# GpSimd waits for VectorE's candidate sums between two of its trees, and three columns of the up-projection move from the end of the selection into the gate table's stage

## The reference: what is computed

```python
def peer_ffn(xn, w_query, sub_keys, expert_u, expert_v):    # for each block of 128 tokens, xb
    q = (xb @ w_query).reshape(c, 8, 2, 128)                 # 8 heads, 2 halves
    s = einsum('chpd,pkd->chpk', q, sub_keys)                # 128 scores per head and half
    s_top, i_top = top_k(s, 16)
    cand = s_top[:, :, 0, :, None] + s_top[:, :, 1, None, :] # sums of pairs
    best, pos = top_k(cand, 16)                              # 16 experts per head
    idx = (i_top half 0 * 128 + i_top half 1) at pos
    g = softmax(best)
    act = gelu(einsum('chkd,cd->chk', expert_u[idx], xb))
    return einsum('chk,chkd->cd', g * act, expert_v[idx])
```

## Time and profile before

| | |
|---|---|
| median of three runs | 3433.51 us |
| the profiled execution: span | 3434.3 us |
| PE busy | 3377.4 us, 98% |
| DVE busy | 2636.7 us, 77% |
| ACT busy | 1240.8 us, 36% |
| POOL busy | 809.2 us, 24% |
| chain that ended last | PE 81%, DVE 14%, DMA 2% |

### The profile page before, as it was taken

How to read it: one execution, slowest core, us unless ns; L and a number is a source line. 1 busy time by engine, 2 the same in 40 slices (tenths; PEclk the granted TensorE clock), 3 DMA queues, 4 the chain that set the end, 5 groups by cost and what they waited for, 6 DMA issues and landing times.

```text
span 3434.3 us, 47304 instructions
## 1 busy us (share of the span) xinstructions
PE 3377.4 (98%) x16086; PEld 2755.3 (80%) x16086; DVE 2636.7 (77%) x5503; ACT 1240.8 (36%) x1980; POOL 809.2 (24%) x661
## 2 busy tenths in 40 slices
PE   7999999999999999999999999999999999999998
PEld 4458855898889988888855688559988888898887
DVE  3574389997888888888736734999978888888888
ACT  2333223794223233333214322339833333222332
POOL 0000026002333333333300000440033333333332
PEclk9999999999999999999999999999999999999999
DMA  4313313468888888888741132144698888888885
GB/s 122 104 37 92 119 37 123 161 254 315 319 304 303 305 304 306 306 308 307 259 159 37 37 103 101 44 140 181 246 354 308 309 308 304 302 306 306 304 305 202
DMA packets 270646, 750.58 MB, mean 219 GB/s; under 512 B 19741, under 2 KB 139293, under 8 KB 243904
## 3 DMA queue, kind: packets, MB, share of 16 engines
q1 hardware_dynamic: 196768, 480.57, 39.7%
q0 software_dynamic: 73760, 268.47, 22.7%
HBM read 681.86 MB, written 67.11 MB: 218 GB/s over the span
## 4 chain that ended last, share of the span: by engine, by line
PE 81%; DVE 14%; DMA 2%; POOL 1%; ACT 1%; issue 1%; SPq 0%; DVEq 0%; POOLq 0%; ACTq 0%
PE ps L1239 29%; PE ps L1225 22%; PE ps L1029 7%; PE ps L898 4%; PE ps L1122 4%; DVE OHS L2143 3%; PE ps L1087 3%; PE ps L876 2%; DVE OHS L2139 2%; PE ps L1205 2%; PE ps L1176 2%; DVE URAWL L2109 1%; PE ps L1008 1%; PE ps L843 1%; PE ps L1044 1%
## 5 line engine op out<-in xcount | busy, mean ns | idle before, releaser
L778 POOL DMA_INDIRECT ROWS<-v_rows_dram,GIS x256 | 331.6, 1295 | 576.8 <-DVE X L2213 484.3
L778 POOL DMA_INDIRECT ROWS<-u_rows_dram,GIS x256 | 300.0, 1172 | 610.5 <-DVE STG L2197 536.3
L1578 ACT ACTIVATE AC<-ps 128x384 f32<-128x384 f32 x192 | 94.5, 492 | 927.8 <-PE ps L1225 927.8
L1239 PE MATMUL ps<-VHI,WHI 128*128 128x512 f32 x1536 | 414.5, 391 | 4.8 <-DVE WLO L2178 2.8
L1239 PE MATMUL ps<-VLO,WHI 128*128 128x512 f32 x1536 | 414.8, 392 | 0.0
L1239 PE MATMUL ps<-VHI,WLO 128*128 128x512 f32 x1536 | 412.1, 390 | 0.0
L1571 ACT CAST VHI<-VRAW 128x512 fp32r<-128x512 f32 x512 | 285.6, 619 | 326.9 <-PE ps L1239 325.6
L2213 DVE SCALAR_TENSOR_TENSOR X<-ROWS,STG,X 128x1024 f32<-128x1024 f32 x256 | 328.3, 1282 | 23.0 <-DMA ROWS<-v_rows_dram,GIS 11.1
L1239 PEld LDWEIGHTS ps<-VLO,WHI 128*128 128x128 f32 x1536 | 288.4, 188 | 63.5
L1239 PEld LDWEIGHTS ps<-VHI,WLO 128*128 128x128 f32 x1536 | 289.0, 188 | 62.3
L1239 PEld LDWEIGHTS ps<-VHI,WHI 128*128 128x128 f32 x1536 | 285.6, 188 | 54.1 <-DVE WLO L2178 3.9
(11 more groups left out here) (281 smaller groups left out, 5352.2 us busy)
## 6 DMA issues: line engine op xcount, KB each, us to landing
VRAW<-v_dram SPq DMA_DIRECT2D x128, 1024.0 KB
URAW<-ut_dram SPq DMA_DIRECT2D x128, 512.0 KB, 3.7
URAW<-ut_dram SPq DMA_DIRECT2D x64, 1024.0 KB, 5.6
g_table<-GST SPq DMA_DIRECT2D x12, 4096.0 KB, 12.6
GT<-g_table SPq DMA_DIRECT2D x62, 768.0 KB, 8.1
WR<-w_in_dram SPq DMA_DIRECT2D x8, 2048.0 KB, 12.1
WR<-w_in_dram SPq DMA_DIRECT2D x32, 512.0 KB, 4.7
WR<-w_q_dram SPq DMA_DIRECT2D x8, 2048.0 KB, 8.0
```

The lines of the kernel that those rows point to most:

```text
L778: pool.indirect_dma_start(out=ROWS[:, k % GR, :], out_offset=None, in_=table, in_offset=bass.IndirectOffsetOnAxis(ap=GIS[:, par, k:k + 1], ...
L1239: last = nc.tensor.matmul(ps[:, 2 + o, :], a[:, par, jj, b * P:(b + 1) * P], c[:, dh, jj, :], start=(first and n == 0), stop=(final and n ...
```

## The change

It has five parts.

1. A semaphore `sums_ready`, to which VectorE adds one behind the candidate sums and the conversion of the indices of each group. GpSimd waits for it ahead of the multiplication of k = 0 of its groups 1 and 2, until the sums of the group after are done.
2. `TAIL_EARLY` goes from 14 to 11 and `LOOP_EARLY` from 6 to 7 (the sum of 11 + 3 x 7 stays 32): 10 columns instead of 13 are computed in the selection's tail, column 10 behind the turning, and 20 instead of 17 beside the slots (160 chunks in 48 slots).
3. `EARLY_BEFORE` goes from 9 to 7: the exponential of group 3 stands four activations behind the group of three, not six.
4. The stores of the table stand behind three and six passes of a round instead of two and five.
5. `dots_done`, `gelu_done` and `gw_ready` become one semaphore, `dot_steps`, with the same waits in effect.

```diff
--- before.py
+++ after.py
@@ -91,9 +91,9 @@
 JG = 4
 NG = NK // JG
 FC = JG - 1
-TAIL_EARLY, LOOP_EARLY = 14, 6
+TAIL_EARLY, LOOP_EARLY = 11, 7
 ESLOTS = 3
-EARLY_BEFORE = 9
+EARLY_BEFORE = 7
 DB = 3
 DT = DB * P
 NOUT = 2 * DB
@@ -396,6 +396,7 @@
     bmax_ready, bexp_ready = lsem("bmax_ready"), lsem("bexp_ready")
     rows_apart, rows_abs, rows_ready = lsem("rows_apart"), lsem("rows_abs"), lsem("rows_ready")
     places_ready, keys_found = lsem("places_ready"), lsem("keys_found")
+    sums_ready = lsem("sums_ready")
     pool_steps = lsem("pool_steps")
     sel_ready, sel_turned = lsem("sel_ready"), lsem("sel_turned")
     ids_staged = lsem("ids_staged")
@@ -417,7 +418,7 @@
     g_loaded = [lsem(f"g_loaded{i}") for i in range(2)]
     u_hi, u_split, u_done = lsem("u_hi"), lsem("u_split"), lsem("u_done")
     v_hi, v_split = lsem("v_hi"), lsem("v_split")
-    stg_ready, dots_done, gelu_done, gw_ready = lsem("stg_ready"), lsem("dots_done"), lsem("gelu_done"), lsem("gw_ready")
+    stg_ready, dot_steps = lsem("stg_ready"), lsem("dot_steps")
     rows_used, gis_ready, pool_went = lsem("rows_used"), lsem("gis_ready"), lsem("pool_went")
     act_ready, wf_ready, whi_ready, w_ready = lsem("act_ready"), lsem("wf_ready"), lsem("whi_ready"), lsem("w_ready")
     v_out, out_added = lsem("v_out"), lsem("out_added")
@@ -667,7 +668,7 @@
                             load_pre(g, g)
                     for m in range(LOOP_EARLY):
                         for s in range(2):
-                            if m == (2, 5)[s]:
+                            if m == (3, 6)[s]:
                                 store_gates(it, s)
                         pass_early(TAIL_EARLY + it * LOOP_EARLY + m)
                 load_pair(1, 1)
@@ -751,6 +752,8 @@
 
                         nc.gpsimd.tensor_tensor(EQ[:, k], *places_and_columns(k), ALU.subtract).then_inc(rows_apart, 1)
                     for k in (1, 0):
+                        if i >= 1 and k == 0:
+                            pool.wait_ge(sums_ready, i + 2)
                         pool.wait_ge(rows_ready, 2 * i + 2 - k)
                         times_keys(nc.gpsimd, i, k).then_inc(pool_steps, 1)
 
@@ -1606,8 +1609,8 @@
                 with act.Fori(0, GSTEPS // 2) as it:
                     step(it, 0)
                     step(it, 1)
-                act.wait_ge(dots_done, GSTEPS)
-                nc.scalar.activation(DOT[:], DOT[:], ACT.Gelu).then_inc(gelu_done, 1)
+                act.wait_ge(dot_steps, GSTEPS)
+                nc.scalar.activation(DOT[:], DOT[:], ACT.Gelu).then_inc(dot_steps, 1)
                 with act.Fori(GSTEPS // 2, (NG - 2) // 2) as it:
                     step(it, 0)
                     step(it, 1)
@@ -2055,6 +2058,7 @@
                             tv[:, :, 1, 0:nb].unsqueeze(2).to_broadcast([P, NS, a1 - a0, nb]), ALU.add))
                     st.did(nc.vector.tensor_copy(TIF[:, i % 2], TI[:]))
                     st.then(dve)
+                    dve.nop().then_inc(sums_ready, 1)
                     cd = [CD[:, h] for h in range(NS)]
                     for h in range(NS):
                         st.did(nc.vector.max(BV[:, h, 0:8], cd[h]))
@@ -2199,7 +2203,7 @@
 
                 def keep_dots(s, par):
                     dve.wait_ge(rows_used, s * GS + (GR + GS))
-                    nc.vector.tensor_copy(DOT[:, bass.ds(s * GS, GS)], STG[:, par, :]).then_inc(dots_done, 1)
+                    nc.vector.tensor_copy(DOT[:, bass.ds(s * GS, GS)], STG[:, par, :]).then_inc(dot_steps, 1)
 
                 def stage_weights(s, par):
                     nc.vector.tensor_copy(STG[:, par, :], GW[:, bass.ds((s - GSTEPS) * GS, GS)]).then_inc(stg_ready, 1)
@@ -2265,9 +2269,9 @@
                     step(it, 0, rows=dot)
                     step(it, 1, rows=dot)
 
-                dve.wait_ge(gelu_done, 1)
-                nc.vector.tensor_tensor(GW[:], DOT[:], GG[:], ALU.mult).then_inc(gw_ready, 1)
-                dve.wait_ge(gw_ready, 1)
+                dve.wait_ge(dot_steps, GSTEPS + 1)
+                nc.vector.tensor_tensor(GW[:], DOT[:], GG[:], ALU.mult).then_inc(dot_steps, 1)
+                dve.wait_ge(dot_steps, GSTEPS + 2)
                 with dve.Fori(GSTEPS // 2, (NG - 2) // 2) as it:
                     step(it, 0, rows=add_row)
                     step(it, 1, rows=add_row)
```

## The result

| | |
|---|---|
| changed kernel, median | 3450.38 us (3448.51 to 3450.5, 4 runs) |
| kernel before, beside it | 3434.4 us (3433.1 to 3436.86, 4 runs) |
| ratio | 1.0049, 95% interval 1.0037 to 1.0062 |
| the profiled execution: span | 3446.5 us (before 3434.3) |

The account below looks back on a forecast made before the run. Two tail chains (TensorE's columns, VectorE's selection) end nearly together, and VectorE paces the slots. Per layer -7.1 (tail) + 7.9 (slots) + 1.1 (clock) = +1.9 us, +3.8 for both: 3437.3 us, range 3430 to 3446.

Parts of the forecast that it names:

- The sums without GpSimd: Selection tail, groups 2 and 3: VectorE's sums without GpSimd beside them save 7.7 us a layer; tail 7.1 us earlier.
- The 0.3 us a group for `BE`: Key search in the tail: VectorE's `BE` comes slightly before GpSimd's tree ends, costing 0.3 us a group (0 to 0.75).
- The idle time and the clock: Turning of the selection and column 10: TensorE idles 8.8 us, its clock falls, +1.1 us a layer (0 to 4.3).
- Three columns into the slots: Gate table's slots: 12.5 us more TensorE work, 5.6 filling waits, 1.0 of waits left; +7.9 us a layer (6.9 to 9.9).
- The 5.6 us of waits: Gate table's slots before: TensorE's 14 waits for one-hot rows, 5.6 us together, which the added column work could at best fill.
- The loads, three columns ahead, keep their lead: Column loads beside the slots: columns come every 2.4 slots instead of 2.8, loads stay in time; cost nothing.
- The second, ScalarE's high halves: Slots: high halves wait for the column two before and block ScalarE's copies; up to 18.4 us together, 3456 us; chance 15%.
- The third: Rival: clock stays low over the whole of column 10, 3.2 us more a layer, 3444 us; chance 13%.
- The first: Rival: VectorE goes on pacing the slots, which grow by only 3.4 us a layer, 3427 us; chance 12%.
- the fourth: Rival: the wait doesn't keep GpSimd off group 3's sums, most of 3.86 us returns a layer, 3441 to 3445; chance 8%.
- The dense stage's beginning: After the slots: the dense stage starts where it did relative to the last column; change 0.

Follow-up runs that it names:

- small_stores: The changed kernel with each gate-table store writing 0.5 MB instead of 4, the dense stage reading the same part at each step: 3426.22 us, ratio 0.9983.

## Why the prediction was wrong, point by point

- **The sums without GpSimd.** Right: 7.5 us a layer sooner at the turning against 7.1. The 0.3 us a group for `BE` didn't come: the tree took 4.85 us and not the 5.38 of the earlier trace rows, and ended with `BE`'s start (555.13 and 555.06). The semaphore instruction behind the conversion, put at nothing with a bound of 0.2 us, showed 0.1 us in each of the four groups.
- **The idle time and the clock.** Right in kind and about in size: 8.36 us idle (8.8 forecast), the turning 1.0 us longer, +0.6 and +1.7 us to the first one-hot product against +1.1. That the mean of the two is so near is luck: the clock came back at different points of column 10.
- **Three columns into the slots: this is the step that failed**, +14.6 and +14.8 us against +7.9. TensorE's own work, 12.5 us more, was nearly right, and so was that TensorE would set the pace: with small stores the chain through the slots is TensorE's behind the first ones. (The prediction's 162.1 us for the stretch before is 161.9 by its own terms, which changes nothing.) The 5.6 us of waits that this work was to fill were replaced by 7.0 us of new ones. Without the late loads the slots take 171.6 us, so they are 4.9 of the 6.7 us that were missing in the sum. The other part is small: one wait of 2.0 us at the first slots, where I had 1.0 us for all waits together, and about 1 us of TensorE's own work (171.6 less 168.6 less 2.0), whose cause stays open.
- **"The loads, three columns ahead, keep their lead"**, which I cost at nothing, is the sentence at fault. I counted the lead in columns, and it is time that a load needs. Beside a store ScalarE now wants the column 7.7 to 8.5 us after the load's issue, and the load takes 11.1 to 11.5. The time of a load beside a store was already used up in the kernel before: its SyncE and ScalarE in order of time have

```profile
681.24 0.33 SPq L645 DMA_DIRECT2D g_table<-GST  x1
683.05 0.34 SPq L632 DMA_DIRECT2D URAW<-ut_dram  x1
```

```profile
694.79 1.05 ACT L1498 CAST UEH<-URAW 128x1024 fp32r<-128x1024 f32 x1 [0.81 <-DMA URAW<-ut_dram]
```

  a load 1.8 us behind a store, and a high half that already waited 0.81 us for it, 11.7 us after its issue. Those rows were there to be read.
- **The rivals.** The second, ScalarE's high halves, named the right instruction but the wrong cause: its waits for the column two before are real (three, 5.7 us) and, by `small_stores`, don't reach TensorE. The order of ScalarE's work costs 2.0 us a layer, but in a place that the rival didn't name, the first slots. The third happened in part: in the second layer the clock stayed low over half of column 10, which cost 0.6 us more than I counted, not 3.2. The first and the fourth didn't happen.
- **The dense stage's beginning**, counted as unchanged, moved by -1.1 and +1.8 us. All versions with full stores lie between 19.7 and 23.1 there, and with small stores it takes 16.6. What moves it within that band stays open.
- The range ended at 3446 and so left out just what happened: its bounds for the slots, 0 to 3 us of waits, rested on the same assumption as the sum.

## What to carry to other kernels

When work is packed closer, recount every prefetch in microseconds: the time from the instruction that frees its buffer to the one that needs it, against the transfer's longest time beside the other traffic, not its median. A hidden transfer whose wait is a few tenths in the trace has no cover left. And where two chains end together, move only as much work as keeps them together: one column moved gave 0.17% where three lost 0.5%, and 0.3% was lost with the column moved but without the wait, because the two gains (a wait on one engine, less work ahead of it on another) need each other.

## What the runs showed of the hardware that was not expected

- A 0.5 MB load that was late took 11.1 to 11.5 us beside a 4 MB store in one queue, and 10.3 to 13.7 us with the store in another, against 4.1 in the median.
- The turning at the lower clock took 2.18 us behind 5.7, 8.4 and 16.1 us of idle time alike: its price did not grow with the idle time's length. Behind 3.2 us of idle time it took 1.20, 1.62, 1.84 and 2.18 us in four cases, so there the clock fell in some and not in others.
- VectorE's two sums, 128x512 each, took 4.17 us beside GpSimd's work where they take 1.16 alone. Its eight `MAX8` took 1.51 us beside GpSimd's multiplication (at 545.71 in the changed kernel) and 1.51 without it (at 470.28): they were not slowed.
